# Where an attention stage takes its spare half units, and the order of a key and query projection

## The reference, cut to what matters

```python
# C: differential attention, 4 heads, two maps of width 32 each
q, k, v = jnp.split(u, [GROUP_W, 2 * GROUP_W], axis=-1)
bias = -slopes[:, None, None, None] * dist
sc = jnp.einsum('bhmqd,bhmsd->bhmqs', qb, k) * scale + bias
p = jax.nn.softmax(sc, axis=-1)
a = (p[:, :, 0] - lam * p[:, :, 1]).astype(v.dtype)
o = jnp.einsum('bhqs,bhsd->bqhd', a, v)
# B: latent attention, 4 heads
q = (rms_norm(c_q, cq_gain) @ w_uq)      # per head 64 plain and 32 rotary columns
kv = (rms_norm(c_kv, ckv_gain) @ w_ukv)  # per head 64 key and 64 value columns
```

## Time and profile before

| | us |
|---|---|
| median of 3 runs | 2891.05 (2889.29 to 2891.29) |
| profiled execution, its own time | 2889.34 |
| its span, first instruction to last | 2887.6 |

### The profile page before, as it was taken

The page is one execution under the profiler, slowest core; times in us unless marked ns, Lnnn a source line. Parts: engine busy times, 40 slices in busy tenths (PEclk is TensorE's granted clock), DMA queues, the critical chain, the costliest instruction groups (busy, mean ns, idle before and its releaser), DMA issues. The chain is left out here.

```text
span 2887.6 us, 36784 instructions
## 1 busy us (share of the span) xinstructions
PE 2674.2 (93%) x13768; PEld 2251.8 (78%) x13768; DVE 1889.1 (65%) x2792; ACT 1375.6 (48%) x2372; POOL 531.7 (18%) x479
## 2 busy tenths in 40 slices
PE   7898989997979999999988989899979799999998
PEld 5677879986858887888776878799868588878887
DVE  3187758766688776445833867687666878864456
ACT  4287347665443222433533863576653423324343
POOL 2187216320000000000022872263100000000000
PEclk9999999998989999999999999999989899999999
DMA  7823337861224444766636232478522244457665
GB/s 218 217 70 86 79 88 240 226 162 52 81 84 144 151 160 163 272 215 197 198 122 175 63 99 59 121 242 223 130 66 73 91 155 151 156 188 257 211 201 171
DMA packets 352300, 437.22 MB, mean 151 GB/s; under 512 B 95734, under 2 KB 225530, under 8 KB 351868
## 3 DMA queue, kind: packets, MB, share of 16 engines
q1 hardware_dynamic: 350396, 433.30, 50.0%
q10 hardware_dynamic: 1728, 1.57, 0.2%
HBM read 290.10 MB, written 142.96 MB: 150 GB/s over the span
## 5 line engine op out<-in xcount | busy, mean ns | idle before, releaser
L2552 PE MATMUL f_ps<-dn_g 128*128 128x512 f32 x2688 | 614.1, 390 | 11.5 <-DVE dn_g L2813 11.5
L2552 PEld LDWEIGHTS f_ps<-dn_g 128*128 128x128 f32 x2688 | 504.1, 188 | 119.3 <-DVE dn_g L2813 9.0
L2813 DVE TENSOR_TENSOR dn_g<-dn_raw,dn_g 128x2048 fp32r<-128x2048 f32 x112 | 256.6, 2292 | 256.5 <-ACT dn_g L2634 256.3
L2634 ACT ACTIVATE dn_g<-dn_raw 128x2048 fp32r<-128x2048 f32 x112 | 214.8, 1918 | 349.3 <-PE f_ps L2552 274.9
L2542 PE MATMUL f_ps<-hc_h,up_w_h 128*128 128x512 f32 x896 | 352.4, 393 | 26.1 <-DVE up_w_l L2779 18.4
L2542 PE MATMUL f_ps<-hc_h,up_w_l 128*128 128x512 f32 x896 | 351.2, 392 | 0.0
L2542 PEld LDWEIGHTS f_ps<-hc_h,up_w_h 128*128 128x128 f32 x896 | 170.2, 190 | 63.0 <-DVE up_w_l L2779 27.7
L1652 DVE TENSOR_REDUCE nmax_ab<-s_ps_ab 128x1 f32<-128x1024 f32 x128 | 156.7, 1224 | 90.9 <-PE s_ps_ab L1541 90.9
L2542 PE MATMUL f_ps<-hc_ld,up_w_h 128*128 128x512 f32 x512 | 201.1, 393 | 0.0
L2542 PEld LDWEIGHTS f_ps<-hc_h,up_w_l 128*128 128x128 f32 x896 | 169.9, 190 | 35.9
L917 DVE CUSTOM_DVE_ANT_0 u_ps_p<-u_ps_p,distance 128x1024 f32<-128x1024 f32 x128 | 157.3, 1230 | 42.3 <-PE u_ps_p L632 39.4
(11 more groups left out here) (344 smaller groups left out, 6041.5 us busy)
## 6 DMA issues: line engine op xcount, KB each, us to landing
act_blocks<-u_stage SPq DMA_DIRECT2D x32, 1792.0 KB, 6.6
dn_raw<-act_blocks SPq DMA_DIRECT2D x112, 512.0 KB, 4.0
mix<-in_w_down SPq DMA_DIRECT2D x128, 256.0 KB, 3.8
down_sums<-mix SPq DMA_DIRECT2D x128, 256.0 KB, 2.7
up_raw<-in_w_up SPq DMA_DIRECT2D x32, 1024.0 KB, 5.6
dn_raw<-down_sums SPq DMA_DIRECT2D x64, 512.0 KB, 5.1
dn_raw<-in_w_down SPq DMA_DIRECT2D x48, 512.0 KB, 4.9
w_raw<-in_w_in SPq DMA_DIRECT2D x16, 512.0 KB, 5.1
```

The lines of the kernel that those rows point to most:

```text
L2552: last = nc.tensor.matmul(f_ps[:, bank0[pi] + i, :], lhs[:, n % 4, 0, q, i * P:(i + 1) * P], rhs[:, n % 4, 1, q, :], start=(down_opens[pi] ...
L2634: nc.scalar.activation(g_h[:, n % 4], dn_raw[:, n % 3], ACT.Copy).then_inc(S["d_hi"], 1)
L2813: nc.vector.tensor_tensor(g_l[:, n % 4], dn_raw[:, n % 3], g_h[:, n % 4], ALU.subtract) \
```

## The change

In `front_stage` the eight half units are placed anew. Half unit 2 is one piece in step 0, 3 is two pieces in steps 2 and 3, 4 is spread by two matmuls over each even step from 6 to 28, 5 is two pieces in steps 31 and 32, and 6 and 7 are one piece each in steps 33 and 34, in the two score banks (`u_ps[:, 0]` and `[:, 1]`), for which they wait until all exponentials are done. ScalarE and VectorE take them in steps 1 (half units 1 and 2), 4, 29, 33, 34 and 35, and half unit 0 ahead of tile 0's maxima and exponentials, where it had come behind them. SP writes half unit 4 after C's third result, and 5 and 6 after the loads of A's first rows. In `rows_stage` the last `turn_back` comes ahead of the second half of unit 7; then B's keys come first (the second pair in bank 0 of `t_ps`), then the swapped rotary columns, then, after the keys' low parts, the rotary columns, the values and the plain queries. ScalarE and VectorE split in the same order. `key_bank` is new.

```diff
--- before.py
+++ after.py
@@ -313,7 +313,9 @@
 
                 def fill_ps(i):
 
-                    return t_ps[:, 2 if i == 1 else 3, :]
+                    return t_ps[:, 2, :] if i == 1 else u_ps[:, i - 6, :] if i >= 6 else t_ps[:, 3, :]
+
+                FILL_AFTER = {2: 1, 3: 3, 4: 4, 5: 5}
 
                 def turned(b):
 
@@ -329,18 +331,16 @@
 
                 def fill_part(n):
 
-                    if n < 2:
-                        return 2, 12 * n, 12 * n + 12
-                    if 4 <= n < 28 and (n - 4) % 6 < 5:
-                        at = (n - 4) % 6
-                        return (n - 4) // 6 + 3, 5 * at, min(5 * at + 5, 3 * KT)
-                    if n in (32, 33):
-                        return 7, 12 * (n - 32), 12 * (n - 31)
+                    if n in (0, 33, 34):
+                        return 2 if n == 0 else n - 27, 0, 3 * KT
+                    if n in (2, 3, 31, 32):
+                        at = 12 * (n % 2) if n < 4 else 12 * (n - 31)
+                        return 3 if n < 4 else 5, at, at + 12
+                    if 6 <= n < 30 and n % 2 == 0:
+                        return 4, n - 6, n - 4
                     return None
 
-                def fill_taken(n):
-
-                    return n if n in (1, 2) else (n - 9) // 6 + 3 if 4 <= n < 28 and n % 6 == 3 else 7 if n == 34 else None
+                FILLS_TAKEN = {1: (1, 2), 4: (3,), 29: (4,), 33: (5,), 34: (6,), 35: (7,)}
 
                 def row_source(r):
                     return rows_first[:, r, :] if r < ROWS_FIRST else v_raw[:, r % 2, :]
@@ -479,16 +479,16 @@
                     spill_fill(3)
                     load_head(2)
                     spill_mix(0)
-                    spill_fill(4)
                     load_head(3)
                     spill_mix(1)
-                    spill_fill(5)
-                    spill_fill(6)
                     spill_mix(2)
+                    spill_fill(4)
                     sp.wait_ge(S["max_done"], 2 * N_ALL)
                     sp.wait_ge(S["fill_done"], 4)
                     for r in range(A_FIRST):
                         sp.dma_start(a_source(r), w[r * P:(r + 1) * P, A0:A0 + 8 * HD]).then_inc(S[f"a_row_landed{r // 2}"], 16)
+                    spill_fill(5)
+                    spill_fill(6)
                     spill_fill(7)
                     spill_mix(3)
                     for j in range(2):
@@ -610,8 +610,10 @@
                         u = LEAD + i // 2
                         if lo == 0:
                             pe.wait_ge(S["w_lo"], u + 1)
-                            if i >= 2:
-                                pe.wait_ge(S["fill_lo"], 1 if i == 2 else i)
+                            if i in FILL_AFTER:
+                                pe.wait_ge(S["fill_lo"], FILL_AFTER[i])
+                            if i >= 6:
+                                pe.wait_ge(S["exp_done"], 2 * N_ALL)
                         for at in range(lo, hi):
                             k, j = at // 3, at % 3
                             wt, x_ = ((u_h, h_hi), (u_h, h_lo), (u_l, h_hi))[j]
@@ -823,13 +825,13 @@
                     unit_weight_high(4)
                     unit_high(2)
                     unit_weight_high(5)
+                    fill_high(0)
                     exponential(0, 0)
                     exponential(0, 1)
                     scale_sum(0)
-                    fill_high(0)
                     for n in range(N_ALL + VALUE_LAG):
-                        if fill_taken(n) is not None:
-                            fill_high(fill_taken(n))
+                        for i in FILLS_TAKEN.get(n, ()):
+                            fill_high(i)
                         if 0 <= n - TURN_LAG < N_ALL:
                             high(n - TURN_LAG, 0)
                         if n + 1 < N_ALL:
@@ -954,14 +956,14 @@
                     dve.sem_inc(S["lam_done"], 1)
                     for u in range(LEAD):
                         unit_low(u)
+                    fill_low(0)
                     maximum(0, 0)
                     maximum(0, 1)
-                    fill_low(0)
                     for n in range(N_ALL + VALUE_LAG + 1):
                         if n + 1 < N_ALL:
                             maximum(n + 1, 0)
-                        if fill_taken(n) is not None:
-                            fill_low(fill_taken(n))
+                        for i in FILLS_TAKEN.get(n, ()):
+                            fill_low(i)
                         if n < N_ALL:
                             weigh(n)
                         if n + 1 < N_ALL:
@@ -1046,6 +1048,9 @@
                 def unit_out(u):
                     return u_ps[:, 2 * (u % 2):2 * (u % 2) + 2, :].rearrange("p a n -> p (a n)")
 
+                def key_bank(j):
+                    return unit_out(1) if j == 0 else t_ps[:, 0, :]
+
                 def head_values(g):
 
                     return B["v_s"][:, :, 4 * g:4 * g + 4, :].rearrange("p e t d -> p t e d")
@@ -1179,8 +1184,8 @@
                     pe.wait_ge(S["row_taken"], 2 * NT - 2)
                     unit_half(0)
                     turn_back(2 * NT - 2)
+                    turn_back(2 * NT - 1)
                     unit_half(1).then_inc(S["unit_done"], 1)
-                    turn_back(2 * NT - 1)
 
                     def query_unit(j, dst):
                         for k in range(2):
@@ -1203,18 +1208,18 @@
 
                     pe.wait_ge(S["bw_lo"], 3)
                     pe.wait_ge(S["back_lo"], 2 * NT)
-                    query_unit(2, t_ps[:, 0, :])
+                    pe.wait_ge(S["row_taken"], 2 * NT)
+                    for j in range(2):
+                        key_unit(j, key_bank(j)).then_inc(S["kv_gemm"], 1)
                     query_unit(3, t_ps[:, 1, :]).then_inc(S["rope_gemm"], 1)
-                    pe.wait_ge(S["row_taken"], 2 * NT)
+                    pe.wait_ge(S["k_lo"], NHEAD)
+                    query_unit(2, t_ps[:, 0, :]).then_inc(S["rope_gemm"], 1)
                     pe.wait_ge(S["unit_lo"], 1)
                     for g in range(2):
                         value_tiles(g, unit_out(g)).then_inc(S["tt_done"], 1)
                     pe.wait_ge(S["rope_done"], 1)
                     for j in range(2):
                         query_unit(j, t_ps[:, j, :]).then_inc(S["q_gemm"], 1)
-                    for j in range(2):
-                        pe.wait_ge(S["tt_lo"], j + 1)
-                        key_unit(j, unit_out(j)).then_inc(S["kv_gemm"], 1)
 
                 @block.scalar
                 def _(act):
@@ -1278,7 +1283,7 @@
 
                     def key_high(e):
                         act.wait_ge(S["kv_gemm"], e // 2 + 1)
-                        nc.scalar.activation(B["k_h"][0:HD, e, :], unit_out(e // 2)[e % 2 * HD:(e % 2 + 1) * HD], ACT.Copy) \
+                        nc.scalar.activation(B["k_h"][0:HD, e, :], key_bank(e // 2)[e % 2 * HD:(e % 2 + 1) * HD], ACT.Copy) \
                             .then_inc(S["k_hi"], 1)
 
                     def head_values_high(g):
@@ -1307,6 +1312,8 @@
                             nc.scalar.activation(u_h[:, :, :], u_raw[:, :, :], ACT.Copy).then_inc(S["w_hi"], 1)
                     back_high(2 * NT - 2)
                     back_high(2 * NT - 1)
+                    for e in range(NHEAD):
+                        key_high(e)
                     act.wait_ge(S["unit_done"], 1)
                     nc.scalar.activation(st_h[:, :], unit_out(0), ACT.Copy).then_inc(S["unit_hi"], 1)
                     head_values_high(0)
@@ -1314,8 +1321,6 @@
                     rope_high()
                     for e in range(NHEAD):
                         query_high(e)
-                    for e in range(NHEAD):
-                        key_high(e)
 
                 @block.vector
                 def _(dve):
@@ -1416,7 +1421,7 @@
 
                     def rope():
                         dve.wait_ge(S["table_landed"], 16 * 2 * NHEAD)
-                        dve.wait_ge(S["rope_gemm"], 1)
+                        dve.wait_ge(S["rope_gemm"], 2)
                         counted(nc.vector.scalar_tensor_tensor(out=roped[:, :], in0=t_ps[:, 0, :], scalar=QK ** -0.5,
                                                                in1=cs[:, 0, :], op0=ALU.mult, op1=ALU.mult))
                         after(nc.vector.scalar_tensor_tensor(out=t_ps[:, 1, :], in0=t_ps[:, 1, :], scalar=QK ** -0.5,
@@ -1438,7 +1443,7 @@
 
                     def key_low(e):
                         dve.wait_ge(S["k_hi"], e + 1)
-                        nc.vector.tensor_tensor(B["k_l"][0:HD, e, :], unit_out(e // 2)[e % 2 * HD:(e % 2 + 1) * HD],
+                        nc.vector.tensor_tensor(B["k_l"][0:HD, e, :], key_bank(e // 2)[e % 2 * HD:(e % 2 + 1) * HD],
                                                 B["k_h"][0:HD, e, :], ALU.subtract).then_inc(S["k_lo"], 1)
 
                     def head_values_low(g):
@@ -1459,6 +1464,8 @@
                         back_low(NT + t - 2)
```

(4 more changed lines are left out.)

## The result

The changed kernel takes 2912.97 us (median of 4 runs, 2910.76 to 2915.38) where the kernel before took 2891.17 beside it: ratio 1.0075, 95% interval 1.0058 to 1.0093. It is slower, by 22 us; 2915 was forecast. The profiled executions differ by 22.8 us of span (2887.6 and 2910.4). The page after, engine shares, answers to the earlier trace rows: TensorE is 11 us busier with the same number of instructions, and VectorE and ScalarE are not.

What follows compares the result with a forecast made beforehand. VectorE and its neighbours bound C's middle, TensorE its end. Layer 0: 6.2 + 8.6 - 1.8 = 13.0; layer 1: 5.2 + 7.6 - 1.8 = 11.0; +24.0 on 2889.34 makes 2913.3, given as 2915 us, range 2901 to 2925.

Steps and rivals of the forecast that it cites:

- What bounds the stage: C's middle: bound by VectorE and its neighbours, half-unit matmuls nearly free there; C's end bound by TensorE.
- The ramp, +8.2 / +7.2: C's start to tile 7: 8.2 us behind in layer 0, 7.2 in layer 1; bounds 6 and 10.
- the clock's in layer 0: Ramp, half unit 2: half clock to about 146, so 9 matmuls slow (3.9 us) and 15 fast (3.5).
- The middle, -2.0: C's tiles 7 to 31: 2.0 us saved a layer from shorter pairs and fewer copies.
- what is saved between the request and tile 16 or 24 goes into that wait: C's middle: savings in n = 12 to 15 and 20 to 23 vanish into waits for the next head's operands.
- nothing goes into the waits: C's middle, the other case: 3.3 us saved a layer in place of 2.0.
- The drain, +8.6 / +7.6: C's end: 48 added matmuls, 11.0 us, less 2.4 of idle, +8.6; layer 1 +7.6 for its clock; bounds 6 to 11.
- B's end, -1.8: B's keys first: last low part 1.8 us sooner a layer despite a 1.6 us wait for `k_lo`; bounds 0 to 3.
- B, the clock falls in the thinned middle: Rival, C's middle: three falls a layer at 2 us each, +12, 2927 us; chance 0.16.
- C: Rival: TensorE bounds C's middle, 16.6 us come off each layer there, 2887 us in all; chance 0.04.
- D: Rival, ramp: staging half free before 125, so the copy holds nobody; 13 us a layer better, 2889; chance 0.03.

Runs made afterwards that it cites:

- middle_empty: Kernel before with only the first and last of 24 matmuls issued in each of half units 3 to 6; 2890.76 us, ratio 0.9993.
- b_only: Kernel before with only the `rows_stage` part of the change (B's new order); 2892.6 us, ratio 1.0003.
- copy0_back: Changed kernel with half unit 0's copy and low part back behind tile 0's exponentials and maxima; 2908.46 us, ratio 1.005.
- five_mid: Kernel before with half units 3 to 7 spread over the middle, five matmuls a step in steps 3 to 27, none in the drain; 2883.96 us, ratio 0.9967.
- both_parts: `five_mid` plus B's keys first, first pair in `t_ps` bank 0, third query unit behind two key lows; 2874.14 us, 0.9937 of before.
- all_three: `both_parts` with the half unit's matmuls put behind `values` in steps 11, 19 and 27; 2871.69 us, 0.9921 of before.
- c_only: Kernel before with only the `front_stage` part of the change; 2912.88 us, ratio 1.0069.

## Why the prediction was right, point by point

**What bounds the stage: right.** `middle_empty` shows directly that half-unit matmuls do not set the middle's pace; that VectorE does is read from its 90% of the stretch. One count was off without harm: of the 72 matmuls that leave the middle's steps, 10 had stood ahead of tile 7, so tiles 7 to 31 lose 62 (86 before, 24 after).

**The ramp, +8.2 / +7.2, measured +7.2 / +6.9.** Counted from half unit 0's copy, tile 1 came 3.8 later than before (3.3 forecast), tile 2 5.2 (6.2), and tiles 2 to 5 cost 1.8, as worked out. The one term that was too large is the clock's in layer 0: half clock ended at 142.4 us (granted 0.68 over 136 to 146), so that 3 of half unit 2's 24 matmuls were slow and not 9. In layer 1 tile 2 came 6.8 later and tiles 5 to 7 gave 1.2 back.

**The middle, -2.0, measured -4.3 / -5.0: the step that failed.** The pairs and the copies were right: tiles 7 to 12 gave 0.73 in layer 0 (0.71 forecast). The failed step is "what is saved between the request and tile 16 or 24 goes into that wait". It holds only if the request stays where it is in the step. It moved 1.15 us up, so the wait shrank from 3.7 to 1.0 us and the savings in steps 12 to 15 and 20 to 23 counted in full. My own bound for "nothing goes into the waits", 3.3, was not enough either, as it didn't let the old waits shrink: 3.3 twice and the 2.7 that the waits lost are the 9.3 measured over both layers. Counted without the two steps across a head boundary (tiles 15 to 16 and 23 to 24, which gave 0.7 and 0.5 in layer 0), the middle gave 3.1 us.

**The drain, +8.6 / +7.6, measured +9.0 / +7.7: right, with two small errors that cancel in part.** The price is the 48 added matmuls, less the idle that they use. They made TensorE 10.5 us busier in layer 0 and not 11.0, and they used 1.5 us of its idle and not 2.4; 2.2 us stayed idle where under 1 was forecast. What the two score banks are worth was not run. The clock of layer 1, 0.92 before, was 1.00 after, as assumed.

**B's end, -1.8, measured -0.4 / -0.65.** The order of waits was right (1.82 us for `k_lo` against 1.6, then 0.73 for `rope`), and `b_only` gave 1.92 in the layer whose clock held, `copy0_back` 1.9. The size was off because the new wait stands where half clock can follow it; I had named the clock for C's stages and not for this one.

**The rivals.** B, the clock falls in the thinned middle, did not happen: 1.00 in both layers of after, and in `middle_empty`. The Trainium skill, "TensorE: Matmul & The Clock Gate" (section "A second HAM failure mode: psum-queue depth-cycling"), tells of a kernel whose short idle gaps between groups of matmuls made the clock swing. These two stretches do not agree with it: the gaps were at most 1.3 us, and no swing is seen. The last tiles of the `five_mid` versions, granted 0.79 to 0.83 in three of six, show that the clock can fall in C's attention all the same. C is refuted by `middle_empty`. D did not happen: the copy came at 135.09. The total came within 2 us partly by luck: the middle won 5.3 us more than forecast and the ramp lost 1.3 less, but B's end won 2.6 less, and 2.5 came in stretches that no step of mine had.

## What to carry to other kernels

Before moving filler work, find for each step what it stands ahead of in its engine's queue: work that is free in busy time can still be dear by delaying the instruction that releases a transfer, and putting it behind that instruction gained 1 to 2 us a layer here. Filler belongs where another engine sets the pace, not in a ramp or drain where the filler's own engine is the last to finish. When a wait is to be covered, look up what its releaser waits for: filling the wait helps nobody if the releaser is on the path, and asking for less of the releaser (two key lows instead of four) does.

## What the runs showed of the hardware

The granted clock stayed at 1.00 over some 90 us of C's middle with TensorE busy for 76.46 of 88.60 us (after) and for 73.72 of 92.30 (`middle_empty`), in short pieces. In tiles 29 to 31, which have no half-unit matmuls in `five_mid`, `both_parts` and `all_three`, it was half for a while in three of six places, and the two tiles took 1.5 us longer there. At B's end it was half from 408.6 to 412.0 in after, behind a wait of 1.82 us, and full behind the same wait of the same length in layer 0 of `b_only` and of `copy0_back`: the code at that place does not decide it alone. The start of `rows_stage` is at half clock in both kernels, but for different lengths; windows views, 293.6 to 297.0 before (full from there), and 302.8 to 309.6 after:

```profile
293.60:297.00 3.40, 3.21 (x8) 2.57 (x9) 0.00 (x0) 0.35 (x1) 0.00 (x0) 0.50 0.67 187
```

```profile
302.80:309.60 6.80, 5.56 (x13) 4.43 (x14) 0.00 (x0) 1.26 (x2) 1.81 (x2) 0.50 0.70 172
```

From the first row matmul to `unit_half(0)` it takes 84.44 us in layer 0 before and 85.31 after, in code that the change leaves as it is; `c_only` has it too (85.30). Layer 1 agrees: the same stretch takes 84.38 us before (granted 0.92 over 1724 to 1745) and 84.25 after (0.91 over 1746 to 1766), but 85.56 in `b_only` (0.84 over 1723 to 1745). So the longer half clock goes with the 0.9 us in each of these places. What sets its length was not settled.
